# A two-layer hybrid block on one core: recurrence levels re-ordered, a small projection packed, two w_ada chunks summed on TensorE

## What is computed

```python
# first layer
ada = silu(c) @ w_ada + b_ada                 # 6 vectors of 1024: shifts, scales, gates
h = modulate(rmsnorm(x, norm_mix), sh1, sc1)
o = token_mixers(h @ w_in, ...)               # gated linear recurrence in both directions + gMLP gating
x = x + g1 * (o @ w_out)
h2 = modulate(rmsnorm(x, norm_ffn), sh2, sc2) # needs sh2, sc2 of ada
x = x + g2 * conv_ffn(h2, w_up, conv_w, conv_b, w_down, rows)
# second layer
proj = rmsnorm_2(x, g_mix) @ w_in             # includes dn_q, dn_k, dn_v and 16 small columns:
fox_f, dn_b, dn_a = 8, 4 and 4 columns        # forget gates, write strengths, decays
...                                           # attention, short convolution, delta rule, FFN
```

## Time and profile before

| | |
|---|---|
| three runs | 949.91, 950.19, 953.58 us (median 950.19) |
| the profiled execution | 950.19 us, of which the traced span is 948.4 us |
| PE busy | 922.4 us, 97% of the span |
| DVE busy | 738.2 us, 78% |
| ACT busy | 477.2 us, 50% |
| SP's loads (q1), share of the 16 DMA engines | 52.1% |
| mean granted clock of PE | 0.993 |

### The profile page before, as it was taken

How to read it: one execution, slowest core, us unless ns; L and a number is a source line. 1 busy time by engine, 2 the same in 40 slices (tenths; PEclk the granted TensorE clock), 3 DMA queues, 4 the chain that set the end, 5 groups by cost and what they waited for, 6 DMA issues and landing times.

```text
span 948.4 us, 19804 instructions
## 1 busy us (share of the span) xinstructions
PE 922.4 (97%) x8596; PEld 868.3 (92%) x8596; DVE 738.2 (78%) x1101; ACT 477.2 (50%) x570; POOL 14.8 (2%) x34
## 2 busy tenths in 40 slices
PE   5999899999999999999999999999999999999997
PEld 3688899999989999999999999999999999999986
DVE  3689997888898989867967886555776997878863
ACT  3454445636546656448755853244546433444363
POOL 0000000002000000000200000000000000000000
PEclk8999999999999999999999999999999999999999
DMA  9998453456447748524553335433355555556541
GB/s 338 350 299 265 136 179 125 142 178 193 151 143 248 254 169 279 198 90 167 197 210 128 123 133 168 154 118 134 128 184 175 184 197 178 179 186 211 179 135 45
DMA packets 114055, 171.89 MB, mean 181 GB/s; under 512 B 3241, under 2 KB 96705, under 8 KB 109873
## 3 DMA queue, kind: packets, MB, share of 16 engines
q1 hardware_dynamic: 111680, 165.63, 52.1%
q0 software_dynamic: 1088, 2.57, 0.8%
q10 hardware_dynamic: 1200, 2.43, 0.7%
HBM read 169.55 MB, written 1.06 MB: 180 GB/s over the span
## 4 chain that ended last, share of the span: by engine, by line
PE 68%; DVE 7%; ACT 2%; issue 2%; DVEq 0%; ACTq 0%
PE bank L1185 21%; PE bank L1186 20%; PE bank L1187 20%; DVE wlo L635 3%; DVE arena L2343 1%; ACT whi L626 1%; PE bank L1772 1%; DVE arena L2432 1%; PE bank L1690 1%; PE bank L1642 1%; PE bank L1763 1%; DVE arena L2009 0%; PE bank L1224 0%; PE bank L1294 0%; PE bank L1660 0%
## 5 line engine op out<-in xcount | busy, mean ns | idle before, releaser
L1185 PE MATMUL bank<-hhi,whi 128*128 128x256 f32 (+1 forms) x1744 | 506.8, 291 | 5.5 <-issue 1.3
L1186 PE MATMUL bank<-hlo,whi 128*128 128x256 f32 (+1 forms) x1744 | 500.1, 287 | 0.0
L1187 PE MATMUL bank<-hhi,wlo 128*128 128x256 f32 (+1 forms) x1744 | 500.1, 287 | 0.0
L635 DVE TENSOR_TENSOR wlo<-raw,whi 128x2048 fp32r<-128x2048 f32 x131 | 299.4, 2288 | 105.9 <-ACT whi L626 83.9
L1185 PEld LDWEIGHTS bank<-hhi,whi 128*128 128x128 f32 x1744 | 334.0, 192 | 14.7 <-issue 10.7
L1186 PEld LDWEIGHTS bank<-hlo,whi 128*128 128x128 f32 x1744 | 334.2, 192 | 4.1 <-issue 1.2
L1187 PEld LDWEIGHTS bank<-hhi,wlo 128*128 128x128 f32 x1744 | 334.1, 192 | 2.5
L626 ACT ACTIVATE whi<-raw 128x2048 fp32r<-128x2048 f32 x131 | 250.2, 1913 | 129.6 <-PE bank L1187 123.7
L1185 PE MATMUL bank<-whi,hhi 128*128 128x256 f32 (+1 forms) x256 | 87.7, 343 | 0.8 <-ACT arena L1145 0.8
L1186 PE MATMUL bank<-wlo,hhi 128*128 128x256 f32 (+1 forms) x256 | 86.6, 338 | 0.0
L1187 PE MATMUL bank<-whi,hlo 128*128 128x256 f32 (+1 forms) x256 | 86.5, 338 | 0.0
(11 more groups left out here) (372 smaller groups left out, 796.4 us busy)
## 6 DMA issues: line engine op xcount, KB each, us to landing
raw<-in_w_up_dram SPq DMA_DIRECT2D x44, 1024.0 KB, 5.1
raw<-in_w_in_tiles_dram SPq DMA_DIRECT2D x32, 1024.0 KB, 4.8
raw<-in_w_down_dram SPq DMA_DIRECT2D x22, 1024.0 KB, 4.9
raw<-in_w_ada_dram SPq DMA_DIRECT2D x19, 1024.0 KB, 6.0
raw<-in_w_in_dram SPq DMA_DIRECT2D x14, 1024.0 KB, 5.8
raw<-in_w_branch_dram SPq DMA_DIRECT2D x6, 1024.0 KB, 5.1
arena<-in_w_ada_dram SPq DMA_DIRECT2D x10, 512.0 KB, 9.5
raw<-in_w_out_dram SPq DMA_DIRECT2D x4, 1024.0 KB, 5.2
```

The costliest lines, as they stand in the source:

```text
L635: dve.tensor_tensor(wlo[:, g % RING, :], raw[:, n % RING, :], whi[:, g % RING, :].bitcast(F32), ALU.subtract).then_inc(w_lo, 1)
L1185: pe.matmul(o, wh, ah, start=start, stop=False, **kw)
L1186: pe.matmul(o, wh, al, start=False, stop=False, **kw)
L1187: return pe.matmul(o, wl, ah, start=False, stop=stop, **kw)
```

## The change

Three things change. The order of work in the recurrence: PE's product v0a is cut into two halves around level 1; ACT's mix of level 1 comes ahead of the split of mv0; on DVE the splits move one step later, `weighted_late(15)` behind level 4 and `weighted_late(16)` behind the gating unit; the list of loads follows. Chunks 17 and 19 are no longer summed on DVE: PE multiplies the raw chunk itself, 128 x 32 pieces against `silu(c)`, into bank 5. The small projection is packed: 32 columns of weights, the eight row tiles spread over four strips of the bank (`smg`), a copy on ACT, and one product with a 0/1 matrix that adds the four strips and puts the rows where they belong (`sm`); around it `conv_start(dq1)`, `conv_dn(dk0)` and `colT` change places.

```diff
@@ the order in which chunks are loaded @@
-    for name in ("ff0", "ff1", "fb0", 8, "fb1", 9, 10, "q0", 11, "q1", 12, 13, 14, "v0", "v1", "mv0", 15, "mv1", 16,
-                 "mu0", "mu1", "gt0", "gt1", 17, "wo0", "wo1", "wo2", 18, "wo3", 19):
+    for name in ("ff0", "ff1", "fb0", 8, "fb1", 9, 10, "q0", 11, "q1", 12, 13, 14, "v0", "v1", "mv0", "mv1", 15, "mu0",
+                 "mu1", "gt0", 16, "gt1", "wo0", "wo1", 17, "wo2", 18, "wo3", 19):
...
+    ADA_DIRECT = (17, 19)
+    def late_sums(c):
+        return sum(a not in ADA_DIRECT for a in range(8, c + 1))
@@ small projection: weights packed to 32 columns, a 0/1 matrix that puts the rows in place @@
-        wsm = slot(18, 1, 0, KT * 96).rearrange("p (k c) -> p k c", c=96)
+        wsm = slot(18, 1, 0, KT * 32).rearrange("p (k c) -> p k c", c=32)
+        sm_place, sm_parts = slot(18, 1, 256, 96), slot(18, 1, 512, T)
@@ SP: what a load waits for when its ring slot held a w_ada chunk @@
-                        last.append([(ada_late, c - 7)])
+                        last.append([(ada_direct, ADA_DIRECT.index(c) + 1) if c in ADA_DIRECT
+                                     else (ada_late, late_sums(c))])
@@ ScalarE, recurrence @@
                 unit_act(f"q{c}", Q[:, 2 * c:2 * c + 2, :], ACT.Silu)
-                split_hi(act, G[f"q{c}"] + RING)
                 if c == 0:
+                    split_hi(act, G["q0"] + RING)
                     tok_keys(0)
-            m_wait("wsT")
-            act.activation(wsT, ...).then_inc(m_empty["act"], 1)
...
             mix_keys(1)
+            split_hi(act, G["q1"] + RING)
+            m_wait("wsT")
+            act.activation(wsT, ...).then_inc(m_empty["act"], 1)
...
             unit_act("mu0", U[:, 0:2, :], ACT.Gelu)
-            split_hi(act, G["mu0"] + RING)
...   (behind the copies of oA and oB)
+            split_hi(act, G["mu0"] + RING)
             unit_act("mu1", U[:, 2:4, :], ACT.Gelu)
@@ ScalarE, second layer @@
+            m_wait("smg")
+            act.activation(sm_parts, m_bank("smg")[:, 0:T], ACT.Copy).then_inc(m_empty["act"], 1)
             conv_start(*dn[0])
             act.wait_ge(*m_done("sm"))
             act.activation(RB[32:36, :], SMY[32:36, :], ACT.Sigmoid)
             link(act.activation(SMA[0:96, :], SMY[0:96, :], ACT.Abs))
+            conv_start(*dn[1])
             link(act.activation(SMA[0:96, :], SMA[0:96, :], ACT.Exp, scale=-1.0))
             act.activation(SMA[0:96, :], SMA[0:96, :], ACT.Ln, bias=1.0).then_inc(sm_ln, 1)
-            conv_start(*dn[1])
@@ TensorE @@
+            def ada_direct_sums(o, c):
+                n = ada_place[c]
+                w = raw[:, n % RING, :].rearrange("p (k n) -> p k n", k=KT)
+                pe.wait_ge(raw_loaded[n % RING], 16 * (n // RING + 1))
+                for nb in range(2):
+                    for k in range(KT):
+                        ins = strip_sums(o, 2 * (c % 4) + nb, w[:, k, P * nb:P * (nb + 1)], silu_c[:, k, 0:1],
+                                         k == 0, k == KT - 1)
+                ins.then_inc(ada_direct, 1)
...
             level(0)
             ada_unit(2)
+            gemm_tok("v0", 512, "v0a", 0, part=(0,))
             level(1)
-            gemm_tok("v0", 512, "v0a", 0)
+            gemm_tok("v0", 512, "v0a", 0, part=(1,))
             level(2)
...
+            ada_direct_sums(bank[5], 17)
             for c in range(2, 4):
                 gemm(f"wo{c}", 512, lo=T)
-            ada_unit(4)
+            pe.wait_ge(ada_late, late_sums(18))
+            for c in (16, 18):
+                for nb in range(2):
+                    strip_sums(bank[5], 2 * (c % 4) + nb, XC[:, c % 8, P * nb:P * (nb + 1)], ones[:, 0:1], True, True)
+            ada_direct_sums(bank[5], 19)
             sum_squares("sum1", 0, T)
...
             for k in range(KT):
-                ins = pe.matmul(o[0:96, 0:T], wsm[:, k, :], HT2[:, T * k:T * (k + 1)], start=k == 0, stop=k == KT - 1)
+                ins = pe.matmul(o[STRIPS[k % 4], 0:T], wsm[:, k, :], HT2[:, T * k:T * (k + 1)], start=k < 4,
+                                stop=k >= 4, skip_group_check=True)
             ins.then_inc(m_full, 1)
-            gemm("dq1", T)
+            gemm("dq1", T, part=(0,))
+            o = m_open("sm")
+            pe.wait_ge(*m_done("smg"))
+            pe.matmul(o[0:96, 0:T], sm_place, sm_parts, start=True, stop=True).then_inc(m_full, 1)
+            gemm("dq1", T, part=(1,))
             gemm("dk0", T)
             gemm("dk1", T)
+            gemm("dv0", T)
...   (the two transposes of colT stand here)
-            gemm("dv0", T)
@@ VectorE, recurrence @@
+            modulation(2, g_wait("A2"), g_empty["dve"])
             level(1)
-            modulation(2, g_wait("A2"), g_empty["dve"])
-            split_lo(dve, G["q1"] + RING)
             values(0, 0)
             level(2)
-            weighted_late(15)
+            split_lo(dve, G["q1"] + RING)
             values(0, 1)
+            level(3)
             split_lo(dve, G["v0"] + RING)
-            level(3)
-            weighted_late(16)
             values(1, 0)
             level(4)
             values(1, 1)
+            weighted_late(15)
             split_lo(dve, G["v1"] + RING)
             level(5)
...   (the splits behind levels 5, 7 and 8 move one step down: mv0's behind level 6, mv1's behind level 8)
-            split_lo(dve, G["mu0"] + RING)
...   (normalised values of the gating unit)
-            weighted_late(17)
+            weighted_late(16)
+            split_lo(dve, G["mu0"] + RING)
             split_lo(dve, G["mu1"] + RING)
...
-                if c == 1:
-                    weighted_late(19)
...
-            modulation(4, g_wait("A4"), g_empty["dve"])
-            dve.wait_ge(*g_done("A4"))
+            dve.wait_ge(ada_direct, 2)
+            modulation(4, bank[5], a4_used)
+            dve.wait_ge(a4_used, 1)
@@ VectorE, second layer @@
             conv_dn(*dn[1])
+            conv_dn(*dn[2])
             dve.wait_ge(sm_ln, 1)
...   (scalings and scans that write RB, then rb_ready)
-            conv_dn(*dn[2])
             conv_dn(*dn[3])
```

More of the change, by code:

```diff
@@ L69, in host_constants @@
         masks[:, lv, 1] = same & right[:, None] & left[None, :]
[L70 to L73, removed]
+    sel = np.zeros((4, 32, 96), np.float32)
+    for col, (row, _, n) in zip((0, 8, 12), SMALL):
+        for j in range(n):
+            sel[:, col + j, row + j] = 1.0
+    return cf, masks.reshape(P, -1), sel.reshape(P, 96)
 SMALL = ((0, 1536, 8), (32, 4616, 4), (64, 4620, 4))
@@ L101, in host_layout @@
     table = np.concatenate(table + [np.repeat(np.repeat(zero, P, axis=1), 5 * P - N_ROWS, axis=0)], axis=0)
-    w_small = np.repeat(np.repeat(zero, 96, axis=1), D, axis=0)
-    for row, c0, n in SMALL:
-        w_small[:, row:row + n] = x["w_in_2"][0][:, c0:c0 + n]
+    w_small = np.repeat(np.repeat(zero, 32, axis=1), D, axis=0)
+    for col, (_, c0, n) in zip((0, 8, 12), SMALL):
+        w_small[:, col:col + n] = x["w_in_2"][0][:, c0:c0 + n]
     w = x["w_in_2"][0]
@@ L211, in build @@
                 ("gt1", "act")]
-    g_units += [(f"wo{c}", "dve") for c in range(4)] + [("A4", "dve")]
+    g_units += [(f"wo{c}", "dve") for c in range(4)]
     for j in range(FFT // 2):
@@ L237, in build @@
     m_units += [("oA", "act"), ("oB", "act"), ("on0", "act"), ("on1", "act"), ("z0", "dve"), ("z1", "dve"),
-                ("sum1", "act"), ("A5", "dve"), ("sum2", "dve"), ("sum3", "act"), ("norm1", "act"), ("sm", "dve"), ("colT", "dve")]
+                ("sum1", "act"), ("A5", "dve"), ("sum2", "dve"), ("sum3", "act"), ("norm1", "act"), ("smg", "act"), ("sm", "dve"), ("colT", "dve")]
     m_units += [(n, "act") for n in ("lk0", "lk1", "sfq0", "sfq1", "sfk0", "sfk1", "rq")]
@@ L433, in build @@
         lv_keys, lv_mixed, lv_spread = sem("lv_keys"), sem("lv_mixed"), sem("lv_spread")
+        ada_direct, a4_used = sem("ada_direct"), sem("a4_used")
         eye_made = sem("eye_made")
@@ L760, in _ @@
             mix_keys(1)
+            split_hi(act, G["q1"] + RING)
+            m_wait("wsT")
+            act.activation(wsT, m_bank("wsT")[:, :].rearrange("p (h q) -> p h q", h=HEADS), ACT.Copy
+                           ).then_inc(m_empty["act"], 1)
             act.wait_ge(lv_upd, 1)
@@ L1300, in ada_unit @@
                 o = g_open(f"A{a}")
-                pe.wait_ge(ada_late, 4 * (a - 1))
+                pe.wait_ge(ada_late, late_sums(4 * a + 3))
                 for c in range(4 * a, 4 * a + 4):
+                    if c in ADA_DIRECT:
+                        continue
                     for nb in range(2):
@@ L1344, in gemm_first, with gemm_tok @@
                             ins.then_inc(g_full, 1)
-            def gemm_tok(name, w, unit=None, t0=0):
+            def gemm_tok(name, w, unit=None, t0=0, part=(0, 1)):
                 wh, wl = w_parts(name, KT)
-                bk = g_open(unit or name)
-                for n in range(2):
```

(12 more changed lines are left out.)

9 lines of the change are left out of this document (4 added, 5 removed).

## The result

The changed kernel takes 953.81 us (median of 14 runs, 952.47 to 957.71), the kernel before beside it 950.46 us (14 runs). The ratio is 1.0031, with a 95% interval of 1.0019 to 1.0044: slower by 0.3%, inside what the prediction calls no change, but above its range (946.0 to 953.0) and 4.0 us over its 949.8. The profiled execution takes 953.92 us, with a span of 952.1 us against 948.4, +3.7 us.

What follows compares the result with a forecast made beforehand. PE's instruction list was taken as the bound (busy 922.4 of 948.4 us). Terms: -4.6 (recurrence) + 4.6 (wo3's load) + 0.55 (clock, tail) - 0.9 (small projection) = -0.35 us, so 949.8 us; 8-in-10 range 946.0 to 953.0.

Steps and rivals of the forecast that it cites:

- The levels: Recurrence: the 2.10 us wait ahead of level 1 and the slow clock behind it go; PE 4.6 us earlier from level 7.
- dearer direct sums: Rival, PE behind wo1 and wo3: direct sums cost 2.6 us a chunk, not 1.3, giving 952.4 us; chance 0.15.
- The transfer: wo3's load lands 5.2 us after leaving SP, though two other transfers follow it at once.
- The small projection: Packed small projection: PE saves 1.8 us, 0.7 more if a wait goes; 0.9 us of gain arrives at fq0.
- the 4.6 us are given back in one wait: PE ahead of wo3: its late load makes PE stand still some 4.4 us, giving back the recurrence's gain.
- The rest down to wo1 is the same list on PE and shifts as a whole.: oA, gt0, z, gt1 down to wo1: all move earlier with the recurrence's 4.6 us, as DVE keeps pace.
- I take the middle, 1.0 us: wo3, behind PE's wait: the clock may fall and cost up to 1.8 us; 1.0 us is taken.
- The sum for the norm waits for the last square anyway: Tail of wo3: the norm's sum waits for the last square, though A4 is complete only at 213.8; region priced +0.0 at full clock.
- 0.45 us of cover: Tail of wo3: between A4's 214.3 and DVE's 214.76, hiding part of the clock's 1.0 us; +0.55 us comes through.
- The two rivals whose number came nearest, 952.4 both: Direct sums at 2.6 us a chunk (chance 0.15); DVE still bounding the levels, only 2 us won there (0.08).
- fg0 lands third, around 207 (one MB more for each transfer at the rate of a median load): Load of fg0 behind wo3's and chunk 19's: its splits bring the wo2 and wo3 residuals to about 211.3, as before.

Runs made afterwards that it cites:

- gate_split: Changed kernel with ACT's split of gt1's weights put back ahead of the squares of oA instead of ahead of mu1's unit; 953.60 us.
- fill_short: Changed kernel with 10 idle products (results not used) between wo2 and wo3, in PE's wait of 4.63 us; 952.68 us.
- direct19_alone: Changed kernel with chunk 17 summed on DVE again, so that PE sums only chunk 19 directly, behind wo3; 950.54 us.
- early17: Changed kernel with chunk 17's direct sum moved from behind wo1 to between the two halves of wo0/wo1; 947.65 us.
- late17: Changed kernel with chunk 17's direct sum moved one block later, from behind wo1 to behind wo2; 961.12 us.
- fill_wait: Changed kernel with 20 idle products (results not used) between wo2 and wo3, which took 8.44 us; 960.61 us.

## Why the prediction was wrong

**What held.** The levels: the wait of 2.10 us and the slow clock behind it went, 4.1 us are won by gt1 (181.31 - 177.21) where I had 4.6. The missing 0.5 us is in v0a: its two halves take 3.06 and 3.24 us (100.10 to 103.16, 103.98 to 107.22), 6.30 in all where I put v0b's 5.85. A direct sum is 1.17 to 1.18 us (predicted 1.3), so the rival "dearer direct sums" is dead; its 128 records are 9 ns apart, 18 ns for each of the 64 products. By the Trainium skill, "TensorEngine Tiling (Array Packing)", section "Instruction Overhead", each would take about 60 cycles, by my estimate 25 ns at 2.4 GHz; the measured 18 ns decide against that here. The transfer: 5.3 us although two others left within 1.4 us; they landed at 9.3 and 11.2 us, one behind the other. The Trainium skill, "DMA: Bandwidth & Descriptors", section "Queues, rings and completion order", speaks of descriptors taken in ring order and of completion that need not be in order; the three landings here came in the order of issue, and no run shows one out of it. The small projection: 0.63 us where I had 0.9, with the wait ahead of dv1 as told (dv1 starts at 461.68; 457.2 + the lag of 4.32 is 461.5).

**What failed.** The step "the 4.6 us are given back in one wait", with the tail behind it, came to +4.2 us net at fg0 where the prediction had +0.55. Its parts, along PE's list:

- *"The rest down to wo1 is the same list on PE and shifts as a whole."* It did not: ACT's moved split put the output gates 1.3 us behind PE, which shows as waits of 0.23 and 0.92 us in wo0. I had followed DVE's list here and not ACT's, though the change moves this split across mu1's unit. gate_split shows it. With the 0.5 us missing from the levels, wo3's load leaves 1.84 us late and wo3 starts 1.94 us late. Cost 1.9 us.
- *"I take the middle, 1.0 us"* for the clock: it was 1.5 (fill_short), within the bound of 1.8. The part of the slow stretch that was to lie in the wait was none in the changed kernel. Cost 0.5 us.
- *"The sum for the norm waits for the last square anyway"*, *"0.45 us of cover"*, and chunk 19's direct sum at nothing. This was a misreading. In the earlier trace rows `ada_unit(4)` starts at 212.15; the norm's sum follows at 212.79 and takes 3.55 us without a wait, ACT's root follows it, and the reciprocal at 217.06 comes right behind that. DVE's split of fa0 at 214.76, which I took for the bound, ended at the same time by chance. PE stood on the path of the tail as much as DVE, so all that it loses there is lost: 0.45 us of cover that wasn't there, and 0.27 + 1.17 - 0.64 = 0.8 us for the sums (direct19_alone: 0.81).
- The small projection, 0.27 us less than told.

1.94 + 0.5 + 0.45 + 0.8 + 0.27 = 4.0 us, of the 4.1 between -0.35 and the +3.7 of the spans. None of the errors was large; all went one way, and my range gave their sum no room. The two rivals whose number came nearest, 952.4 both, were wrong in their reasons: the direct sums are cheap, and the levels gave 4.1 us.

A second path failed beside PE's: *"fg0 lands third, around 207 (one MB more for each transfer at the rate of a median load)"*. By the median of 5.2 us for a MB the rule gives 201.0 + 2 x 5.2 = 211.4, not 207, and fg0 landed at 210.2. Its splits and the residuals behind them put DVE's split of fa0 at 217.94 to 220.23, where it ended at 217.05 before. The reciprocal waited for PE for only another 1.0 us, until 221.25. So of the 4.2 us at the norm only 1.0 could have been had by PE alone, from the clock and the sums; the other 3.2 us hang on the late loads as well, which is what early17 removes for both paths at once.

## What to carry to other kernels

A load's slot is freed by whoever reads it last. Handing that read to the busiest engine, in its program order, ties the load to that engine's progress: look for the place in its list where the read can stand soonest, at best in a wait that is there already (one call moved: 6 us). When time is won upstream, walk every engine's list over the same stretch, not only that of the two that were edited on purpose; a split moved past a unit put wo3's load off by 1.35 us, more than the direct sum itself (1.18). And before something is costed at nothing because "another engine is later", check in the trace which of the two ends coincide by chance: follow the last wait back one more link.

## What the runs showed of the hardware

- The low clock is not tied to the wait's length alone. In the changed kernel, with 4.63 us of wait, it began at 208.4 and lasted to 211.8; with 4.49 us, in gate_split, it began at 205.0 and lasted to 211.9. In late17 (10.56 us) it began at about 205.7, 0.9 us into the wait (lengths from the mean clock of a row: 0.86 of full is 0.28 us at half):

```profile
205.00:206.00 1.00, 0.00 (x0) 0.00 (x0) 0.00 (x0) 0.00 (x0) 0.00 (x0) 0.86 0.04 6
206.00:217.00 11.00, 1.58 (x7) 1.61 (x8) 3.08 (x3) 3.43 (x3) 0.00 (x0) 0.50 0.98 317
```

  wo3 then took 7.41, 8.20 and 7.65 us instead of 5.9. So nearly the same wait cost 1.5 or 2.3 us more behind it; what fixes the moment of the fall isn't settled by these runs. The Trainium skill, "TensorE: Matmul & The Clock Gate", section "Part 1: The HAM clock gate", says that the chip judges its activity in windows that run free of the kernel; the differing starts agree with that, but no run here moves one to show it.
- In fill_wait PE stood still for 2.6 us in the middle of chunk 19's direct sum, for nothing that the profile shows, while the queue that loads instructions moved two packets. Behind it the granted clock fell again (0.83 from 222 to 232), and the norm's sum took 5.24 us instead of 3.55. That makes up the run's span: wo3's end 2.1 us later than in the changed kernel, 2.8 for the stop, 1.7 for the clock, 6.6 us in all, as the spans say (958.7 against 952.1). Where the stop comes from wasn't tried.

```profile
217.96 1.21 PE L1308 MATMUL bank<-small,raw 128*32 128x1 f32 x124
221.76 0.23 PE L1308 MATMUL bank<-small,raw 128*32 128x1 f32 x4 [2.59 <-issue]
```
